# One encoder block with product-key experts: three-tile segments, eight row slots, a later pick, weights on ScalarE

## The reference

```
h = rmsnorm(x);  proj = h @ w_in                       # gated linear attention + windowed attention inputs
x = x + (g_gla * (gla(...) @ w_gla_out) + g_swa * (swa(...) @ w_swa_out)) @ w_out
q = (rmsnorm(x) @ w_q) -> 8 heads x 2 halves; scores = q . sub_keys (128 keys for each half)
vals, idx = top_k(scores, 16);  cand = vals0[:, None] + vals1[None, :]       # 256 candidates
top_vals, pos = top_k(cand, 16); eidx = cidx[pos]; gates = softmax(top_vals)
x = x + sum over heads and k of gates * gelu(h . u[eidx]) * v[eidx]          # 16384 experts
x = x + sigmoid(rmsnorm(x) @ w_ple_gate) * (p @ w_ple_proj);  return rmsnorm(x)
```

## Time and profile before

| | us |
|---|---|
| median of three runs | 3672.26 |
| lowest and highest | 3670.47, 3678.3 |
| the profiled execution, its own time | 3678.36 |
| its span, first to last instruction | 3676.6 |

### The profile page before, as it was taken

The page is one execution under the profiler, slowest core; times in us unless marked ns, Lnnn a source line. Parts: engine busy times, 40 slices in busy tenths (PEclk is TensorE's granted clock), DMA queues, the critical chain, the costliest instruction groups (busy, mean ns, idle before and its releaser), DMA issues.

```text
span 3676.6 us, 34347 instructions
## 1 busy us (share of the span) xinstructions
PE 2804.1 (76%) x10748; PEld 1882.9 (51%) x10748; DVE 2717.2 (74%) x5983; ACT 1129.9 (31%) x2427; POOL 1321.9 (36%) x1028
## 2 busy tenths in 40 slices
PE   8879878847887788787988788796776676675555
PEld 6767756735554455564654446563443443443112
DVE  0143988898778887778777877778777877788884
ACT  2223343222324332324233342333232332323211
POOL 0010434234344444224334444324344444334551
PEclk9989989868998899898998899897888888787777
DMA  6576989979999999989999999989999999999996
GB/s 208 182 257 249 420 333 356 386 301 389 421 421 408 405 392 421 414 328 381 421 421 413 393 404 421 421 327 385 421 421 414 422 421 421 408 380 419 422 421 253
DMA packets 198985, 1388.05 MB, mean 378 GB/s; under 512 B 22658, under 2 KB 24578, under 8 KB 35091
## 3 DMA queue, kind: packets, MB, share of 16 engines
q0 software_dynamic: 147456, 1073.81, 71.6%
q1 hardware_dynamic: 51346, 312.04, 21.7%
HBM read 1368.99 MB, written 16.78 MB: 377 GB/s over the span
## 4 chain that ended last, share of the span: by engine, by line
DMA 34%; PE 31%; DVE 18%; issue 11%; ACT 5%; POOL 2%; SPq 0%; DVEq 0%; POOLq 0%; ACTq 0%
DMA uv<-in_uv,idx 31%; PE bank L535 12%; PE bank L545 9%; DVE acc L1239 6%; PE ysum L723 5%; DVE uv L1207 3%; POOL uv L492 2%; PE bank L604 2%; DMA slab<-in_slabs 2%; DVE lidx L1061 1%; ACT bufX L799 1%; DVE bufX L1026 1%; DVE vals L1058 1%; ACT bufX L756 1%; DVE sm L1030 1%
## 5 line engine op out<-in xcount | busy, mean ns | idle before, releaser
L492 POOL DMA_INDIRECT uv<-in_uv,idx x1024 | 1321.7, 1291 | 2290.2 <-DVE acc L1239 1284.4
L1207 DVE SCALAR_TENSOR_TENSOR uv<-uv,hbuf 128x1024 f32<-128x1024 f32 x1024 | 1250.0, 1221 | 421.0 <-DMA uv<-in_uv,idx 400.2
L723 PE MATMUL ysum<-uv,diag 128*128 128x512 f32 x1708 | 1001.2, 722 | 530.3 <-ACT diag L960 501.8
L723 PEld LDWEIGHTS ysum<-uv,diag 128*128 128x128 f32 x1708 | 351.2, 221 | 1029.6 <-ACT diag L960 688.3
L1239 DVE SCALAR_TENSOR_TENSOR acc<-uv,dots,acc 128x1024 f32<-128x1024 f32 x597 | 763.2, 1278 | 10.5 <-DVE acc L1239 0.9
L535 PE MATMUL bank<-bufA,slab 128*128 128x256 f32 (+1 forms) x2400 | 446.7, 346 | 1.7 <-ACT bufB L756 1.7
L535 PEld LDWEIGHTS bank<-bufA,slab 128*128 128x128 f32 x2400 | 399.9, 198 | 79.3 <-issue 40.9
L960 ACT ACTIVATE diag<-ident,dots 128x128 f32<-128x128 f32 x427 | 170.3, 399 | 755.6 <-DVE dots L1226 740.2
L545 PE MATMUL bank<-slab,bufA 128*128 128x256 f32 x1408 | 323.3, 390 | 3.5 <-DMA slab<-in_slabs 2.8
L952 ACT ACTIVATE dots<-dots 128x2 f32<-128x2 f32 x512 | 103.6, 202 | 708.2 <-DVE uv L1207 705.3
L545 PEld LDWEIGHTS bank<-slab,bufA 128*128 128x128 f32 x1408 | 276.4, 197 | 66.6 <-issue 24.4
(11 more groups left out here) (137 smaller groups left out, 2449.2 us busy)
## 6 DMA issues: line engine op xcount, KB each, us to landing
slab<-in_slabs SPq DMA_DIRECT2D x255, 1024.0 KB
uv<-in_uv,idx POOLq DMA_INDIRECT x1024
acc<-x_d SPq DMA_DIRECT2D x8, 512.0 KB, 12.7
hbuf<-h_d SPq DMA_DIRECT2D x8, 512.0 KB
x_d<-acc SPq DMA_DIRECT2D x8, 512.0 KB
bufC<-in_x SPq DMA_DIRECT2D x3, 1024.0 KB, 9.0
bufA<-in_x SPq DMA_DIRECT2D x3, 1024.0 KB, 11.4
x_d<-bufA SPq DMA_DIRECT2D x3, 1024.0 KB
```

Of the source, the lines that this page charges most:

```text
L492: nc.gpsimd.indirect_dma_start(out=uv[:, at % NS, :], out_offset=None, in_=a["uv"], in_offset=bass.IndirectOffsetOnAxis(ap=idx[:, g % 4, k ...
L723: ins = mm(ysum[:, c, :], diag[:, m % DS, :], uv[:, at % NS, D + c * 512:D + c * 512 + 512], start=(m == first), stop=(m == last))
L1207: v.scalar_tensor_tensor(out=row, in0=row, scalar=1.0, in1=hbuf[:, i % HB, :], op0=ALU.mult, op1=ALU.mult, accum_out=dots[:, g % 3, k:k + ...
```

## The change

Seven things change together.

1. `SEGS` becomes 1, 2, 2, 3: four segments instead of five. `GROUPS` becomes (0,1), (2,3), (4,5,6), (7), and two groups are hosted, in segments 2 and 3. 204 slabs are loaded instead of 255. All buffers of a segment grow to three tiles.
2. `NS` goes from 10 to 8 slots and `HB` from 2 to 1. With one `hbuf`, SP loads the next tile's at the tile's own first step, after the last dot of the tile before. `acc` is loaded five steps ahead.
3. `ON_PE`: tile 0 gives PE 38 rows, tiles 1 to 4 as before 61, tiles 5 to 7 three of four, 92 each. In all 558 rows instead of 427.
4. `AHEAD` is 12. Head 0's pick is made in one go at step -5, right behind `wq1` of segment 0, which is at -7.
5. In the two segments that host a tail, the stages behind `wq1` follow every second step. The tail that no segment hosts keeps its place at steps 452 to 459, now for three tiles.
6. The product with the shares moves from DVE to ACT: two `ACTIVATE` with a scale for each step, behind the gelu, which ACT waits for.
7. The sums of squares for the second norm and the final norm move from DVE to ACT.

In the new order `wq1` is at steps -7, 50, 178 and 306, and `wq8` at 0, 57, 206 and 334. Segment 3 (tiles 5 to 7) has 80 stages in steps 209 to 334, and no stage of a segment is left behind 336.

```diff
-SEGS = (1, 2, 2, 2, 1)
+SEGS = (1, 2, 2, 3)
-NS = 10
-HB = 2
+NS = 8
+HB = 1
-AHEAD = 2 * STEPS
+AHEAD = 12
+AT_ONCE = -5
-ON_PE = [(), ODD, ODD, ODD, ODD, ODD, ODD, ODD]
+MOST = tuple(k for k in range(TOPK) if k % 4)
+ON_PE = [(1, 4, 7, 10, 13), ODD, ODD, ODD, ODD, MOST, MOST, MOST]
-GROUPS = ((0, 1), (2, 3), (4, 5), (6,), (7,))
-HOST = {0: 2, 1: 3, 2: 4}
+GROUPS = ((0, 1), (2, 3), (4, 5, 6), (7,))
+HOST = {0: 2, 1: 3}
@@ plan
-        due = PER_TILE * AT[s] - AHEAD - 2
+        due = PER_TILE * AT[s] - AHEAD - 2 if s else AT_ONCE - 2
+        gap = 2 if s in GUEST else 1
-            step = begin + i * (due - begin) // last if i <= last else due + i - last
+            step = begin + i * (due - begin) // last if i <= last else due + gap * (i - last)
-            begin = max(found[-1][0] + 1, PER_TILE * (tiles[-1] + 1) + 4)
+            begin = max(found[-1][0] + 3, PER_TILE * (tiles[-1] + 1) + 4)
@@ SP
-                i, at = divmod(n + 10, PER_TILE)
+                i, at = divmod(n + 5, PER_TILE)
-                i, at = divmod(n + (10 if HB > 1 else 0), PER_TILE)
+                i, at = divmod(n + (5 if HB > 1 else 0), PER_TILE)
@@ ACT
+                    square_sums(junk, [(x1[:, t, :], stat_h[:, 0, t:t + 1]) for t in range(tt)])
...
+                    square_sums(junk, [(x2[:, t, :], stat_t[:, 0, TT + t:TT + t + 1]) for t in range(tt)])
...
-            def gelu(n):
+            def weights(n):
                 fn(part, part, ACT.Gelu_apprx_tanh).then_inc(gelu_done, 1)
+                if n % STEPS == 0:
+                    act.wait_ge(share_step, 2 * g + 2)
+                act.wait_ge(gelu_done, n + 1)
+                for k in (2 * at, 2 * at + 1):
+                    m = fn(dots[:, g % 3, k:k + 1], dots[:, g % 3, k:k + 1], ACT.Copy, scale=gexp[:, g % 4, k:k + 1])
+                m.then_inc(wts_done, 1)
...
-                    gelu(n - 1)
-                g, at = divmod(n, STEPS)
-                if at == 4 and 0 <= g + 2 < NHEAD:
-                    peer_exp(g + 2)
+                    weights(n - 1)
+                m, at = divmod(n + AHEAD - 4, STEPS)
+                if at == 0 and 1 <= m < NHEAD:
+                    peer_exp(m)
+                if n == AT_ONCE + 1:
+                    peer_exp(0)
@@ DVE
-                    for t in range(tt):
-                        step(v.scalar_tensor_tensor(out=h2[:, t, :], in0=x1[:, t, :], scalar=1.0, in1=x1[:, t, :],
-                                                    op0=ALU.mult, op1=ALU.mult, accum_out=stat_h[:, 0, t:t + 1]))
...
             def topk_at(n, at):
-                m, within = divmod(2 * n + at, TOPK)
-                if 0 <= m + 2 < NHEAD:
+                m, within = divmod(2 * (n + AHEAD) + at, TOPK)
+                if 1 <= m < NHEAD:
...
+                if (n, at) == (AT_ONCE, 0):
+                    for piece in range(TK):
+                        topk(0, piece)
+                    numbers(0)
...
-                    if at == 0 and 0 <= n - 1 < END:
-                        weights(n - 1)
```

More of the change, by code:

```diff
@@ L1104, in stage @@
                     step(v.tensor_tensor(x1[:, 0:tt, :], x1[:, 0:tt, :], h2[:, 0:tt, :], ALU.add))
-                    settle()
-                    for t in range(tt):
-                        step(v.scalar_tensor_tensor(out=h2[:, t, :], in0=x1[:, t, :], scalar=1.0, in1=x1[:, t, :],
-                                                    op0=ALU.mult, op1=ALU.mult, accum_out=stat_h[:, 0, t:t + 1]))
                 elif n == "rt":
@@ L1123, in stage @@
                     step(v.tensor_tensor(x2[:, 0:tt, :], x2[:, 0:tt, :], tp[:, 0:tt, :], ALU.add))
[L1124 to L1128, removed]
                 elif n == "T2":
@@ L1190, in topk_at @@
             def topk_at(n, at):
-                m, within = divmod(2 * n + at, TOPK)
-                if 0 <= m + 2 < NHEAD:
+                m, within = divmod(2 * (n + AHEAD) + at, TOPK)
+                if 1 <= m < NHEAD:
                     if within < TK:
-                        topk(m + 2, within)
+                        topk(m, within)
                     elif within == TK:
-                        numbers(m + 2)
+                        numbers(m)
+                if (n, at) == (AT_ONCE, 0):
+                    for piece in range(TK):
+                        topk(0, piece)
+                    numbers(0)
             def dot(at):
@@ L1218, in shares @@
                                     ).then_inc(share_step, 1)
[L1220 to L1227, removed]
             def add_row(at):
@@ L1271, in _ @@
                         stage(s, name)
-                g, at = divmod(n, STEPS)
-                if at >= 6 and 0 <= g + 2 < NHEAD:
-                    shares(g + 2, at - 6)
+                m, at = divmod(n + AHEAD, STEPS)
+                if at >= 6 and 1 <= m < NHEAD:
+                    shares(m, at - 6)
+                if n in (AT_ONCE + 2, AT_ONCE + 3):
+                    shares(0, n - AT_ONCE - 2)
                 i, at = divmod(n - 2, PER_TILE)
```

## The result

| | before | changed |
|---|---|---|
| median | 3671.36 us (4 runs) | 3738.59 us (4 runs) |
| lowest, highest | 3669.73, 3678.3 | 3735.61, 3742.32 |

The ratio is 1.0179 (95% interval 1.0166 to 1.0193): 1.8% slower. The forecast said slower by 0.8%, 3700, in a range of 3620 to 3785. Direction and range held; the size did not: 28 us were forecast and 67 measured, 2.4 times as much.

A forecast was written before the change was run, and what follows sets the result against it. DMA was taken to bound most stretches, with PE back to back in the two-tile query stretches. Terms -24 + 10 - 15 + 139 - 3 - 111 + 38 = +34 gave 3711, about 3706 as median, written 3700; range 3620 to 3785.

The forecast's parts named there:

- Start: Before step 0: first gather at about 240, first dot at about 257 instead of 309; segment 1 starts at the same clock time.
- Steps 0 to 63: First stretch: segment 1's first scores at 721, step 64 at 815 instead of 839, a gain of 24 us.
- Steps 64 to 175: DMA-bound stretch, 690 us: -10 for query stages drifting out, +20 for holes from the shorter ring, a loss of 10.
- The ring over all: Eight slots: a gather may take 10.0 us and still fits; holes cost 20 us in steps 64 to 175, 7 at the tail.
- Rival C: The ring starves if a gather's latency passes 10.0 us; at 11, +130 us, in all 3790; chance 0.15.
- One `hbuf`: At seven tile boundaries DVE waits 7 to 10 us for the load, costing 5.5 us each: a loss of 38.
- Steps 208 to 303: Three-tile segment: PE takes the bound from DMA, 10.4 us a piece, 735 us against 596, a loss of 139.
- Steps 304 to 335: Three-tile queries, spread: DVE some 210 us, PE 195, DMA 192; 228 against 231, a gain of 3.
- Steps 336 to 511: No segment left: 928 us against 1038.8, a gain of 111, with 12 added for the three-tile tail and 7 for the ring.
- The end: Behind the last step: the tail of tile 7 is unchanged at 47.7 us.
- The sum: All stretches with the `hbuf` loss: +34 us on the profiled span, to 3711, about 3706 as median, written as 3700.
- rival D: Last tiles: with 1.5 rows a step, PE at its lower clock needs 5.1 us against DMA's 4.98; 3735, chance 0.09.

The follow-up runs named there:

- run 11: The changed kernel with the rows on PE of before (none of tile 0, odd ones elsewhere): 3709.21 us, ratio 1.0101.
- run 2: The changed kernel with segments 1, 2, 2, 2, 1, the tail groups of before, ten slots and two `hbuf`: 3619.58 us, ratio 0.9863.
- run 1: The changed kernel with segments 1, 2, 2, 2, 1 and the tail groups of before, still eight slots and one `hbuf`: 3710.34 us, ratio 1.0109.
- runs 3 and 10: The kernel before with eight slots instead of ten, 3727.74 us, and with nine instead of ten, 3689.53 us.
- run 3: The kernel before with eight slots instead of ten, nothing else: 3727.74 us, ratio 1.0152.
- run 4: The kernel before with one `hbuf` instead of two, still ten slots: 3703.85 us, ratio 1.0095.
- run 5: The changed kernel with half of the terms in the three-tile segment's weight products, output not the reference's: 3577.63 us in a single execution.
- run 13: The changed kernel with the three-tile segment's stages behind `wq1` every third step instead of every second: 3719.30 us, ratio 1.0131.

## Why the prediction was right or wrong

*Start.* Right: first dot at 255.5 for 257, and segment 1 bound to the same clock time.

*Steps 0 to 63.* "The last six to seven steps at 5.3 each lead to step 64 at 815" is a wrong sum: 793 and six to seven times 5.3 are 825 to 830, and 828.6 was measured. That the steps of the working meet it is luck in part. The first scores were at 714 for 721. Behind them the query steps took 10.6 each for 10.2, and the last six 7.5 each for 5.3, with the 7.7 us for `hbuf` in them. And "What PE gains falls partly into its waits, so I take +20" hides two errors: against run 11 the rows delay the first scores by 35 us (714 and 680), more than half of the 52, while the rest of the change brings them 21 earlier (701 before).

*Steps 64 to 175.* 705.5 for 691.2. Without the short ring and with two `hbuf` it is 677 (run 2) where the term gives 680, so this part was right. The two together cost 14 to 19 us there (changed kernel and run 1), and not 25.5.

*The ring over all.* I gave it about 27 us with the tight tail; runs 3 and 10 measure 57 on the kernel before. The 20 for steps 64 to 175 was near (18); what failed is that the others got 7 in all, where 176 to 207, 208 to 303 and 336 to 463 lose 6, 18 and 15. The bare latency was bounded by 2.49 and 9.0; the first gather of the changed kernel, with none ahead of it, took 5.9 us, the shortest 5.4. The Trainium skill (DMA: Bandwidth & Descriptors, Anatomy of one DMA) gives about 2.0 us plus bytes by 436e3, an estimate of 4.4 us for a row. The measured 5.4 to 5.9 decides; and that a short ring would cost nothing, which the forecast drew from the 4.4, falls with run 3. Rival C, the starving ring, was wrong at eight slots and is what happens at seven. Its price was also worked out for a turn of 19.9 us, where eight slots have one of 14.95.

*One `hbuf`.* 38 in the sum, 33 measured alone (run 4), with waits of 7.6 us on average for 7 to 10: right.

*Steps 208 to 303.* 740.5 for 736.1, and the bound is PE, as run 5 shows. The 10.4 us piece is 10.36, PE is busy 90% for "above 90%", at clock 0.95 as stated, and the DMA rate is 335 for 345.

*Steps 304 to 335.* "228 against 231" was wrong by 23, with the wait 233.5 for 256.2. I compared sums over 32 steps (DVE 210, PE 195, DMA 192) and added little to the largest. The busy times came out near (DVE 195, PE 211), so no engine was full in 256 us; what failed is the path. The work of a query stage goes from PE to DVE to ACT and back to PE, one turn takes 31.5 to 34.5 us for four steps, and the sum has no term for it. Run 5 with shorter pieces and run 13 with more steps to a turn each give 22 back. Both would do so too if the ring alone were too short for a piece of 10.4 us. The loop stands in the trace; its share against the ring's wasn't measured.

*Steps 336 to 511.* 939 for 953, and two errors met. "I add 12" for the bunched tail was too small: steps 448 to 463 took 150.8 us, where DMA's 92 and the 12 make 104. The term had the four long stages, too small (68 us for steps 456 to 459), and nothing for the store and load of three tiles, for which steps 452 and 453 take 25 us. The other 160 steps were 33 under the forecast; at 427 GB/s instead of 421 a row takes 2.46 us, which is 11 of it, and the rest is open.

*The end.* 53.4 for 48, or 51.1 by the cut of rows 2, not traced.

*The sum.* By stretches it is off by -1.5, +9.6, -14.3, -1.5, -4.4, +22.7, +14.0 and +5.4, in all 30 us. It stood at 3706 and I wrote 3700, against my own terms; with that and the wrong sum for step 64, some 16 to 21 of the 39 us between 3700 and 3739 are slips and no mechanism. And rival D was wrong: the last tiles with 1.5 rows a step on PE ran at DMA's rate, at a granted clock of 0.84 instead of 0.81.

So the start, the three-tile stretch and `hbuf` came out in mechanism and size. What failed are the 815, the 228 for a stretch whose bound is a loop and no engine, and the 12 for the tail; the too high price in steps 64 to 175 hid a part of it.

## What to carry to other kernels

A change of seven parts is seven forecasts: here parts worth -50 and -37 lay under others worth +57, +33, +28 and +24. Where two streams are joined in a fixed order, don't stop at the engines' sums over a stretch. Follow one stage's work from engine to engine until the first engine may go on, and set that turn against what the DMAs need for its steps (here 31.5 to 34.5 us against 25). And before slots are paid for larger tiles, price one slot: the first cost 16 us and the second 38 on the kernel before, and one more 179 on the changed kernel.

## What the runs showed of the hardware

A 1 MB gather with none ahead of it took 5.9 us from the start of its instruction to landing (the first of the changed kernel; the shortest of all 5.4), 9.6 to 10 in a full queue. The gathers of tile 7 ran at 427 GB/s in the changed kernel and all kernels made from it with three-tile segments and eight slots, where all kernels with two-tile segments gave 419 to 422. The times of steps 480 to 495 and 496 to 511 go the same way, 79.2 and 76.3 us against 80.5 and 78.1 in the kernel before. What makes that difference is open.
